# Attention of a diffusion block on one core: scores with keys on the partitions instead of turned probabilities

## What is computed

```
q  = (c_q @ w_uq).reshape(B, S, 16, 64 + 32);  q_rope = apply_rope(q[..., 64:])
kv = (c_kv @ w_ukv).reshape(B, S, 16, 64 + 64); k_nope, v = kv[..., :64], kv[..., 64:]
for qs in range(0, S, 128):
    s = (q_nope . k_nope[:qe] + q_rope . k_rope[:qe]) * 96 ** -0.5
    s = where(causal, s, -inf)
    p = softmax(s)                       # over keys
    outs.append(p @ v[:qe])
```

## Time and profile before

| | |
|---|---|
| time, median of 3 | 3292.61 us (3290.19 to 3294.17) |
| profiled execution: its time, its span | 3288.14 us, 3286.3 us |
| granted TensorE clock over the span | 0.938 |
| busy share over the span | PE 86%, DVE 47%, ACT 29%, POOL 10% |
| the attention stage | 1523.8 to 1891.3 us of the span |
| in that stage, busy | PE 338.99, DVE 203.33, ACT 147.13, POOL 40.91 us of 367.50 |

### The profile page before, as it was taken

The page is one execution under the profiler, slowest core; times in us unless marked ns, Lnnn a source line. Parts: engine busy times, 40 slices in busy tenths (PEclk is TensorE's granted clock), DMA queues, the critical chain, the costliest instruction groups (busy, mean ns, idle before and its releaser), DMA issues. The chain is left out here.

```text
span 3286.3 us, 43025 instructions
## 1 busy us (share of the span) xinstructions
PE 2810.2 (86%) x16707; PEld 1828.7 (56%) x16709; DVE 1558.9 (47%) x2502; ACT 940.0 (29%) x1565; POOL 321.4 (10%) x388
## 2 busy tenths in 40 slices
PE   5999879797999999999999995797878757988785
PEld 3678678575888878865555574332223552322231
DVE  3148868558777766754555556111111670111114
ACT  6112322245323225445433332111010540110014
POOL 0000045300000000120111000011110001111100
PEclk8999989898999999999999997898989878998997
DMA  7511200212223238540000124999999649999996
GB/s 295 202 51 38 77 1 1 115 52 90 96 97 109 98 130 271 189 155 7 7 7 4 52 100 196 394 419 424 422 422 403 243 176 380 417 424 420 424 414 251
DMA packets 196700, 663.63 MB, mean 202 GB/s; under 512 B 42039, under 2 KB 83070, under 8 KB 142734
## 3 DMA queue, kind: packets, MB, share of 16 engines
q1 hardware_dynamic: 178062, 627.26, 48.7%
q0 software_dynamic: 18432, 33.60, 2.7%
HBM read 614.36 MB, written 79.95 MB: 211 GB/s over the span
## 5 line engine op out<-in xcount | busy, mean ns | idle before, releaser
L3100 PE MATMUL psum<-moe_ring,hreg 128*32 128x512 f32 x3200 | 386.4, 640 | 97.1 <-DMA moe_ring<-in_moe_w 95.4
L3100 PEld LDWEIGHTS psum<-moe_ring,hreg 128*32 128x32 f32 x3200 | 120.5, 117 | 358.6 <-issue 286.2
L3206 DVE TENSOR_TENSOR ex_hb<-ex_sil,psum 128x256 f32<-128x256 f32 x64 | 27.0, 421 | 585.4 <-ACT ex_sil L3179 585.4
L1349 PE MATMUL psum<-gu_hi,x1r 128*128 128x512 f32 x712 | 226.6, 394 | 9.3 <-DVE x1r L1476 5.0
L1702 PE MATMUL psum<-dn_op 128*128 128x512 f32 x924 | 210.2, 389 | 4.3 <-DVE dn_op L1797 4.3
L1702 PEld LDWEIGHTS psum<-dn_op 128*128 128x128 f32 x924 | 173.2, 188 | 41.2 <-DVE dn_op L1797 5.4
L3179 ACT ACTIVATE ex_sil<-psum 128x256 f32<-128x256 f32 x64 | 24.5, 383 | 574.9 <-PE psum L3100 574.9
L3152 PE MATMUL psum<-moe_ring,hreg 128*32 128x512 f32 x1536 | 173.2, 605 | 14.4 <-issue 11.8
L1349 PE MATMUL psum<-gu_hi,gu_er 128*128 128x512 f32 x504 | 158.6, 389 | 0.0
L1349 PEld LDWEIGHTS psum<-gu_hi,x1r 128*128 128x128 f32 x712 | 135.4, 190 | 39.4 <-DVE gu_lo L1472 7.9
L3219 DVE COPY ex_y<-psum 128x512 f32<-128x512 f32 x64 | 44.3, 692 | 221.0 <-PE psum L3152 206.6
(11 more groups left out here) (636 smaller groups left out, 5657.8 us busy)
## 6 DMA issues: line engine op xcount, KB each, us to landing
moe_ring<-in_moe_w SPq DMA_DIRECT2D x280, 1024.0 KB
x<-in_moe_w SPq DMA_DIRECT2D x96, 1024.0 KB
x<-in_w_down SPq DMA_DIRECT2D x77, 256.0 KB, 3.0
x<-midrow SPq DMA_DIRECT2D x77, 256.0 KB, 3.4
XF<-in_w_ada SPq DMA_DIRECT2D x16, 1024.0 KB
moe_ring<-yrow SPq DMA_DIRECT2D x16, 1024.0 KB, 12.4
xrow<-x SPq DMA_DIRECT2D x24, 512.0 KB, 2.6
x<-xrow SPq DMA_DIRECT2D x24, 512.0 KB, 9.6
```

The lines of the kernel that those rows point to most:

```text
L1349: last = pe.matmul(ps[4 * (u % 2) + BANK[i]][:, :], weight(u, i, w)[:, k, :], x[i][:, k, :], start=k == 0 and n == 0, stop=k == 3 and n == 2)
L3100: last = pe.matmul(ps[i][r, :], xT[i][:, k, r], ring[slot_of(n)][:, j, kk * 512:(kk + 1) * 512], start=k == 0, stop=k == KD - 1)
```

## The change

Scores are now computed twice. A **first pass** uses only the high parts (`Qh`, `Kh`, in `fp32r`), with queries on the partitions as before, and only its row maxima are kept (`nmx`). TensorE turns the eight maxima of a group of four tiles into two rows (`shifts`), ScalarE writes these as rows 96 and 97 of the high queries (`shifts`, `m_ev`), and a one in row 96 or 97 of the high keys adds them. A **second pass** (`exponents`) then makes, for each block k of 128 keys, the shifted scores with keys on the partitions, by three `fp32r` products (high-high, high-low, low-high); ScalarE's exponentials (`weights`) land directly in the layout that `apply` takes. The probabilities and the sums are no longer turned. Instead VectorE adds the blocks up (`add`), TensorE multiplies the sum by a matrix of ones (`divisors`, 64 equal rows for each head), VectorE inverts the 128x512 result (`reciprocal`) and multiplies it in (`output`).

A pair is two units: u even (tiles 0 to 3, 4 key blocks) and u odd (tiles 7 to 4, 8 key blocks). In a step (u, k) TensorE does the second pass of block k for both heads, then what `bank_turns()` puts there (first-pass scores of the next unit, keys or queries of the next pair, shifts), then `apply` of the block before, and at k = 1 the `divisors` of the unit before. The queries of the two heads now have one layout, so VectorE multiplies them by the tables in two parts (32 and 96 rows), GpSimd adds the parts (`rotate`), ScalarE rounds to the high part and VectorE subtracts for the low part (`low`). Keys are split likewise. `latents` turns 5 sources of 128 columns instead of 7.

```diff
+    for p in range(HEAD_PAIRS):
+        u, n = 2 * p, p + 1
+        rest = score_items(u + 1)[EARLY:]
+        turns[u, 0], turns[u, 1], turns[u, 2], turns[u, 3] = rest[0:2], rest[2:4], rest[4:], [("m", u + 1, 0)]
+        if n < HEAD_PAIRS:
+            turns[u + 1, 0], turns[u + 1, 1], turns[u + 1, 2] = [("k", n, 0)], [("q", n, 0)], [("q", n, 1)]
+            small, large = score_items(u + 2), score_items(u + 3)[:EARLY]
+            turns[u + 1, 4], turns[u + 1, 5] = small[:4], small[4:]
+            turns[u + 1, 6], turns[u + 1, 7] = [("m", u + 2, 0)] + large[:1], large[1:]
...
+                def rotate(p, w):
+                    pool.wait_ge(q_ev, 2 * p + w + 1)
+                    x = Q[p % 2][64:96, w, :]
+                    pool.drain()
+                    pool.tensor_tensor(x, x, turned[64:96, :], ALU.add).then_inc(q_sum, 1)
...
-                    kind, p, i = TURNS_[n - 2]
+                    kind, p, i = order[n - 2]
                     if kind == "s":
-                        pe.wait_ge(ex, NI * p + i + 1)
+                        pe.wait_ge(mx, scored[order[n - 2]] + 1)
...
-                def turn(p, i):
...
-                            last = pe.transpose(ps[4 + b // 4][:, (k - b) * P:(k - b + 1) * P], PR[m % 3][:, k * P:(k + 1) * P], ident)
...
+                def shifts(n, u):
+                    pe.wait_ge(mx, max(scored["s", u, i] for i in range(8)) + 1)
+                    for j in range(4):
+                        last = pe.matmul(bank(n)[96:98, j * P:(j + 1) * P], nmx[:, u % 2, j, :], ident, start=True, stop=True)
+                    last.then_inc(item, 1)
...
+                def exponents(u, k, w):
+                    p, J = u // 2, blocks_before(u) + k
+                    if k == 0:
+                        pe.wait_ge(m_ev, u + 1)
+                        pe.wait_ge(q_lo, 2 * p + w + 1)
+                        pe.wait_ge(k_ev, p + 1)
...
+                    if J >= 1:
+                        pe.wait_ge(ex, 2 * (J - 1) + w + 1)
...
+                    for x, y, z in ((Kh, Qh, 0), (Kh, Ql, 1), (Kl, Qh, 2)):
+                        last = pe.matmul(S[:, c:512], x[p % 2][w][:, key], y[p % 2][:, w, q], start=z == 0, stop=z == 2 and not diagonal)
...
+                def divisors(u):
+                    pe.wait_ge(added, blocks_before(u) + blocks_of(u))
+                    if u >= 1:
+                        pe.wait_ge(inverse, u)
+                    for w in range(2):
+                        last = pe.matmul(ps[7][64 * w:64 * w + 64, :], one[:, :], acc[:, w, :], start=True, stop=True)
+                    last.then_inc(sm, 1)
...
+                def queries(p, w):
+                    n = at["q", p, w]
+                    dve.wait_ge(item, n + 1)
+                    if 2 * p + w >= 1:
+                        dve.wait_ge(q_sum, 2 * p + w)
+                    dve.tensor_tensor(turned[64:96, :], bank(n)[96:P, :], K.CS[96:P, :], ALU.mult)
+                    dve.tensor_tensor(Q[p % 2][0:96, w, :], bank(n)[0:96, :], K.CS[0:96, :], ALU.mult).then_inc(q_ev, 1)
...
+                def add(u, k):
+                    J = blocks_before(u) + k
+                    c = span(u, k)[0]
+                    dve.wait_ge(ex, 2 * J + 2)
+                    if k == 0 and u >= 1:
+                        dve.wait_ge(sm, u)
...
+                def output(u):
+                    dve.drain()
+                    dve.wait_ge(sm, u + 1)
+                    dve.reciprocal(R[:, :], ps[7][:, :]).then_inc(inverse, 1)
+                    dve.drain()
+                    dve.wait_ge(raw, u + 1)
+                    x = OF[:, u // 2, u % 2 * 512:u % 2 * 512 + 512]
+                    dve.tensor_tensor(x, x, R[:, :], ALU.mult)
```

More of the change, by code:

```diff
@@ L2342, in _, with keys @@
+                apply(*before)
+                divisors(NU - 1)
             @block.scalar
             def _(act):
[L2344 removed]
+                def keys(p):
+                    n = at["k", p, 0]
                     act.wait_ge(item, n + 1)
[L2346 to L2351 removed]
@@ L2374, in _ @@
-                done = []
-                for n, (kind, p, i) in enumerate(TURNS_):
-                    if kind == "k":
-                        keys(n, p)
-                    elif kind == "s":
-                        if len(done) >= 2:
-                            copy_turned(*done[-2])
-                        weights(n, p, i)
-                        done.append((p, i))
-                copy_turned(*done[-2])
-                copy_turned(*done[-1])
+                    for w in range(2):
+                        last = act.activation(Kh[p % 2][w][0:64, :], bank(n)[64 * w:64 * w + 64, :], ACT.Copy)
@@ new lines, in _ @@
+                for w in range(2):
+                    last = act.activation(Kh[0][w][64:P, :], K.KR[64:P, :], ACT.Copy)
+                last.then_inc(rows_hi, 1)
+                keys(0)
+                queries(0, 0)
+                queries(0, 1)
+                shifts(0)
+                for u in range(NU):
+                    for k in range(blocks_of(u)):
+                        weights(u, k, 0)
+                        weights(u, k, 1)
+                        for kind, a, i in turns.get((u, k), []):
+                            if kind == "k":
+                                keys(a)
+                            elif kind == "m":
+                                shifts(a)
+                        for kind, a, i in turns.get((u, k - 1), []):
+                            if kind == "q":
+                                queries(a, i)
+                        if k == 0 and u >= 1:
+                            output(u - 1)
@@ L2436, in _ @@
-                copy_turned(*done[-2])
-                copy_turned(*done[-1])
-                divisors(*done[-1])
-                output(*done[-1])
+                dve.wait_ge(rows_hi, 1)
+                for w in range(2):
+                    last = dve.tensor_tensor(Kl[0][w][64:P, :], K.KR[64:P, :], Kh[0][w][64:P, :].bitcast(F32), ALU.subtract)
+                last.then_inc(rows_lo, 1)
+                keys(0)
+                queries(0, 0)
+                queries(0, 1)
+                low(0, 0)
@@ L2442, in attention_output @@
+                add(*before)
+                output(NU - 1)
 def attention_output(nc, K, A, R):
```

404 lines of the change are left out of this document (220 added, 184 removed).

## The result

The changed kernel took 3368.41 us (median of 4 runs, 3364.75 to 3369.85), the kernel before 3292.66 (4 runs): ratio 1.0229, 95% interval 1.0211 to 1.0247. The direction was right, the forecast size a little over half of the measured one.

A forecast was written before the change was run, and what follows sets the result against it. TensorE was taken to set the attention stage's pace. Opening, first pair, six pairs and last pair made 409.3 us against 366.5 (+42.8); with −2 in `latents`, net +41, about 3333 us, range 3304 to 3358.

The forecast's parts named there:

- the walk's zero: Start point of the step-by-step count through a pair: where VectorE ends the last maximum of an odd unit.
- The walk through a pair: Attention pair followed step by step: 48.05 us at full clock, VectorE working 38.4 and waiting 9.6, against 45.3 before.
- What TensorE gives and takes: TensorE's work in an attention pair: 24.2 us out, 21.1 in, leaving about 37, 3 less than before.
- VectorE's sum: VectorE's work in an attention pair: 39.4 us, about 38.4 after overlap, with two reciprocals of 3.2 each.
- The rival of a reciprocal at 0.69: Attention's reciprocal runs at copy speed, 0.69 us: pairs 45.5 at full clock, total 3299, up to 3312; chance 0.12.
- The waits: VectorE's idle times in an attention pair, for scores, keys, `sm`, GpSimd's sum and others: 9.6 us in all.
- a rival of chance 0.1: Half clock for whole pairs, total 3400; also GpSimd and VectorE slowing each other at query sums, 3 to 6 us.
- The clock in the hole: TensorE, nearly idle 7 us in a pair, falls to half clock; maxima come 1.9 us later, pair 49.9.
- Opening, pair 0, last pair: Ends of the attention stage: opening 28.6 us at half clock, first pair 48.0, last pair 33.3.
- `latents`: Stage where two of seven turned sources go, saving evictions and turnings: −2 us, between 0 and −2.8.
- The rival of half clock for whole pairs, or of contention, at 3400: TensorE at half clock for whole attention pairs, 10 us a pair, or GpSimd and VectorE slowing each other; chance 0.1.
- the likeliest case: Whole kernel, with half clock once in each pair: 3333 us, on its own 3322 to 3350; chance 0.5.

The follow-up runs named there:

- e5: Changed kernel plus six TensorE matmuls whose results nobody reads, as fill in its waits before the second and third small scores; 3355.6 us, ratio 1.0210.
- e2: Changed kernel with the reciprocal of the sums replaced by a copy of the same shape, outputs scaled wrongly; 3360.3 us, ratio 1.0215.
- e3: Changed kernel with only the high-high product in the second pass, the two with low parts left out; 3354.5 us, ratio 1.0195.
- e15: On top of e5, GpSimd writes its zero rows in the opening only after its wait for `rows_lo`; 3353.4 us, ratio 1.0190.
- e12: On top of e5, one more bf16 matmul of 128 columns adding zeros behind each second-pass group without a mask; 3357.7 us, ratio 1.0197.
- e8: Changed kernel with e3's single second-pass product, plus fill of 3 and 4 unread matmuls in TensorE's waits; 3334.6 us, ratio 1.0134.
- e16: Changed kernel with the first two small maxima right behind the output, plus 2 unread matmuls in each of three TensorE waits; 3355.7 us, ratio 1.0197.
- e4: Changed kernel with a second buffer for the turned query halves, so head 1's products need not wait for GpSimd's sum; 3361.0 us, ratio 1.0215.
- e10: Changed kernel with e4's second buffer, plus 4 unread matmuls in TensorE's second wait only; 3346.3 us, ratio 1.0160.

## Why the prediction was right in kind and half in size

The stage was forecast at 409.3 us and took 455.9. By the prediction's own terms: opening 28.6, measured 34.6; pair 0 48.0, measured 52.3; six pairs at 49.9, measured 55.2 on average, 31.8 in all; last pair 33.3, measured 37.8. (These are cut at the walk's zero, the end of the last maximum that VectorE takes in an odd unit: 1560.75, 1613.05 and 1944.25.) That is 46.6 too little (6.0, 4.3, 31.8 and 4.5), and the 10 us by which the later stages are shorter hid a fifth of it.

**The walk through a pair** had the right links. Cut at the same places and with the clock out of it (e5, VectorE's timeline from 1776.63 to 1829.90), it compares so:

| link | forecast | e5 |
|---|---|---|
| last maximum of the odd unit to the copy | 4.9 | 6.4 |
| copy to last maximum of step 1 | 4.1 | 4.1 |
| to the query product of head 0 | 11.2 | 11.95 |
| to that of head 1 | 5.1 | 6.1 |
| to the last small maximum | 16.4 | 17.2 |
| to the last maximum of the odd unit | 6.35 | 7.55 |
| sum | 48.05 | 53.3 |

With half clock the forecast was 49.9 and the changed kernel took 54.7.

- **What TensorE gives and takes: the step that failed.** "TensorE has about 37 us of work in a pair, 3 less than now": it has 44.1, about 2 more than before. The slots that I took from rows of long runs of equal products do not hold in short, mixed groups. By starts in e5's timeline: second pass with masks 16.2 (forecast 13.4), first pass with masks 7.5 (5.1), `apply` 9.4 (8.0), the rest 11.0 (10.3). A first product behind a mask or an `apply` takes 0.31 to 0.34 where 0.23 stands in a row; 128 columns take 0.11 to 0.16 in the second pass, not 0.067 (0.06 stands only where they follow 512 columns of the same query in the first pass). "The upper end is 2.4 us a pair, little of it where TensorE is waited for" was wrong twice: the excess is 7 us, and the first, third and last links, which wait for TensorE in the rows, are 3.4 longer than forecast (1.5, 0.75, 1.2). Some 2 of the 7 stand in the kernel before too: by the same prices it has 40 us of work in a pair, and its window shows 42.3, so the prices could have been seen to be low before the change.
- **VectorE's sum** was right: 38.9 us a pair in the window, forecast 38.4; the reciprocal 3.357, forecast 3.2 from three short rows. By the 8 repeats of the Trainium skill ("VectorE: DVE Perf Modes"), as the prediction estimated, it would have been 4.3; the rows were right. The rival of a reciprocal at 0.69 is out. VectorE's busy share is 70% and not 80 because the stage is longer.
- **The waits** stood where they were named: for `sm` at the copy (3.2, forecast 2.4), for keys and `sm` (1.9 + 2.1, forecast 3.5), for GpSimd (2.3, forecast 1.2 to 1.5). What I left out is that VectorE and GpSimd slow each other in SBUF. GpSimd's sum took 3.4 where I had 2.6, the low parts 1.42 and 1.35 for 1.22: 1.1 us a pair on the fourth and fifth links. With 2 in the opening that is about 10 in the stage; I had 3 to 6, inside a rival of chance 0.1. The rest of the fifth link, about 0.5, is waits for two more scores of TensorE (0.35 and 0.21).
- **The clock in the hole.** It fell to 0.50 inside the wait of 4.3 us that follows the one of 2.5, for 7 us, as forecast, and costs 1.4 a pair where I had 1.9. That it answers to an edit (7 us of half clock, 10 in e2, 35 in e3) I had not foreseen.
- **Opening, pair 0, last pair.** Opening and pair 0: forecast 76.6, measured 86.9. In the opening TensorE's queries of head 1 wait 4.6 us for the bank of the keys, which the walk missed, and then run at half clock; VectorE's first two low parts run beside GpSimd (4.45 for 2.44; with e15 the opening was 1.5 shorter). Pair 0 is 2.9 shorter than the average of the next six, forecast 2; its first link is 2.9, as forecast, and the others exceed the forecast much as in the pairs behind it. Behind the copy nothing is saved: what VectorE has less to do there went into a wait of 6.4 us for keys. The last pair has the first link's 1.5 too, and VectorE waits 3.7 us in all for its last exponentials and divisors; the rest of its 4.5 I have not traced.
- **`latents`**: −2.1, forecast −2. The sum has no term for the stages after attention, and they came out 10 us shorter. That the total lies nearer to the forecast than the stage does is luck.

The rival of half clock for whole pairs, or of contention, at 3400, was a little nearer (32 us off, against 35) than the likeliest case, and yet neither of its mechanisms is the main one: the largest share, about 4 of the 5.2 us by which a pair at full clock is longer than forecast, is waits for TensorE, whose own slots are longer. That the slots make these waits is worked out from the rows; the runs bear it out in size: 1.0 us of slots added in e12 made the pair 0.6 longer, 8.3 taken away in e8 made it 4.0 shorter, so half of the excess of 7 is 3.5.

## What to carry to other kernels

Take a matmul's price from rows in the mix in which it will stand: here short groups that alternate in type, width and mask cost a quarter more than the forecast from long runs, 33.1 us for 26.5, and this turned a saving of 3 us a pair into a loss of 2. Adding up the window of the kernel before by the same prices would have shown part of it. A wait in the timeline is a place to look, not the cause: when moving it leaves the period the same (e16), look at the engine that runs through that stretch almost without a pause. And hold the clock up with matmuls in the waits before judging an edit of a few microseconds; without that, e3's and e4's pairs scattered by 10 and 2 us, where differences of 4.0 (in e8, from one pair) and 1.9 (in e10) could be read with it.

## What the runs showed that I had not expected

- Half clock followed the kernel's edits: about 7 us in a pair of the changed kernel, 10 with the shorter wait of e2, over 35 at a time with less work for TensorE (e3), none with fill in the waits (e5).
- Two engines in SBUF: GpSimd's sum of 32x1024 takes 2.36 us beside a reciprocal that reads PSUM and 3.38 beside an addition of VectorE in SBUF; VectorE's subtraction of 96x1024 takes 1.21 and up to 3.36, its product of 512 columns 0.69 and 2.19.
- The stages after attention, whose code did not change, ran 10.3 us shorter, mostly in two waits that the profile puts down to no other engine. The cause stays open.
